# A decoder trunk on one core: ScalarE scales a step's output rows behind the high parts of keys and scores, and VectorE forms the last row sums

## The reference

```python
h = rmsnorm(x, norm_g); proj = h @ w_in            # ten projections
u = conv3(c_a * x_a) + conv_b                      # short convolution branch
y_a = (b_a * u * silu(z_a)) @ w_a_out
# retention branch: 4 heads, chunks of 128 positions, per-head decay
s = (q @ k.T) * decay_in;  o_in = s @ v
cross = (q @ state) * xi
state = state * chunk_decay + (k * zeta).T @ v     # carried from chunk to chunk
o = o_in + cross
o = o * rsqrt(mean(o * o) + EPS)                   # per row of 512
y_b = (o * silu(z_b)) @ w_b_out
x = x + (sigmoid(g_a) * y_a + sigmoid(g_b) * y_b) @ w_o
out = rmsnorm(x, final_g)
```

## Time and profile before

| | |
|---|---|
| median of three runs | 1357.13 us |
| the profiled execution's own time | 1357.46 us |
| its span | 1355.7 us |
| TensorE busy | 1344.5 us, 99% |
| VectorE busy | 1101.8 us, 81% |
| ScalarE busy | 621.2 us, 46% |
| GpSimd busy | 381.1 us, 28% |
| granted TensorE clock, mean | 0.998 of full speed |

### The profile page before, as it was taken

How to read it: one execution, slowest core, us unless ns; L and a number is a source line. 1 busy time by engine, 2 the same in 40 slices (tenths; PEclk the granted TensorE clock), 3 DMA queues, 4 the chain that set the end, 5 groups by cost and what they waited for, 6 DMA issues and landing times.

```text
span 1355.7 us, 18174 instructions
## 1 busy us (share of the span) xinstructions
PE 1344.5 (99%) x6930; PEld 1150.3 (85%) x6930; DVE 1101.8 (81%) x1179; ACT 621.2 (46%) x844; POOL 381.1 (28%) x411
## 2 busy tenths in 40 slices
PE   9999999999999999999999999999999999999997
PEld 8788888888888899888888888888888888888886
DVE  6898575688888888789999998748776998788887
ACT  7843243433333343333434443448778433434445
POOL 0100112344444554333343342225444001100002
PEclk9999999999999999999999999999999999999999
DMA  9746477877677777778888889878878699945443
GB/s 337 217 132 215 139 218 225 263 204 204 200 216 230 218 233 229 255 245 273 281 273 274 273 291 291 251 219 252 265 220 266 155 326 304 232 157 202 163 86 125
DMA packets 134630, 310.35 MB, mean 229 GB/s; under 512 B 9488, under 2 KB 54160, under 8 KB 125456
## 3 DMA queue, kind: packets, MB, share of 16 engines
q1 hardware_dynamic: 123024, 260.41, 54.4%
q0 software_dynamic: 11376, 48.76, 19.6%
q10 hardware_dynamic: 144, 0.02, 0.0%
HBM read 241.00 MB, written 59.77 MB: 222 GB/s over the span
## 4 chain that ended last, share of the span: by engine, by line
PE 91%; ACT 2%; DVE 2%; DMA 2%; issue 2%; POOL 1%; SPq 1%; POOLq 0%; ACTq 0%; DVEq 0%
PE psum L2747 13%; PE psum L2745 13%; PE psum L2748 13%; PE psum L2888 7%; PE psum L2889 7%; PE psum L2890 7%; PE psum L2663 5%; PE psum L2665 5%; PE psum L2664 5%; PE psum L2652 3%; PE psum L2655 3%; PE psum L2654 3%; PE psum L2790 2%; PE psum L2792 2%; PE psum L2791 2%
## 5 line engine op out<-in xcount | busy, mean ns | idle before, releaser
L1210 ACT ACTIVATE slots<-work 128x1024 fp32r<-128x1024 f32 (+1 forms) x182 | 182.1, 1009 | 404.8 <-PE psum L2748 147.7
L2747 PE MATMUL psum<-hc,slots 128*128 128x512 f32 x784 | 305.2, 389 | 0.0
L2745 PE MATMUL psum<-hc,slots 128*128 128x512 f32 x784 | 305.2, 389 | 0.0
L2748 PE MATMUL psum<-hc,slots 128*128 128x512 f32 x784 | 305.1, 389 | 0.0
L1503 ACT ACTIVATE last_slot<-arena 128x1024 fp32r<-128x1024 f32 x112 | 118.6, 1062 | 163.0 <-PE psum L2890 156.5
L2888 PE MATMUL psum<-last_slot 128*128 128x512 f32 (+1 forms) x452 | 175.3, 388 | 0.0
L2889 PE MATMUL psum<-last_slot 128*128 128x512 f32 (+1 forms) x452 | 175.0, 387 | 0.0
L2890 PE MATMUL psum<-last_slot 128*128 128x512 f32 (+1 forms) x452 | 175.0, 387 | 0.0
L2748 PEld LDWEIGHTS psum<-hc,slots 128*128 128x128 f32 x784 | 147.2, 188 | 30.8
L2745 PEld LDWEIGHTS psum<-hc,slots 128*128 128x128 f32 x784 | 147.2, 188 | 29.4
L2747 PEld LDWEIGHTS psum<-hc,slots 128*128 128x128 f32 x784 | 147.2, 188 | 29.3
(11 more groups left out here) (230 smaller groups left out, 2753.6 us busy)
## 6 DMA issues: line engine op xcount, KB each, us to landing
work<-w_channel SPq DMA_DIRECT2D x99, 512.0 KB, 5.7
hx<-hx_scratch SPq DMA_DIRECT2D x32, 1024.0 KB, 8.9
work<-w_channel POOLq DMA_DIRECT2D x59, 512.0 KB, 7.1
arena<-w_last SPq DMA_DIRECT2D x19, 1024.0 KB, 7.8
hx<-hx_scratch SPq DMA_DIRECT2D x32, 512.0 KB, 6.4
qk<-qk_scratch SPq DMA_DIRECT2D x32, 512.0 KB, 4.5
arena<-w_last POOLq DMA_DIRECT2D x9, 1024.0 KB, 11.2
v_raw<-value_scratch SPq DMA_DIRECT2D x32, 256.0 KB, 4.9
```

Of the source, the lines that this page charges most:

```text
L1210: nc.scalar.activation(slots[:, u % SLOTS, 0, 0:columns_of(u)], src, ACT.Copy, scale=-1.0 if negated(u) else 1.0).then_inc(w_hi, 1)
L2745: nc.tensor.matmul(bank, slot[:, 0, w], x_high, start=product in STARTS and j == 0, stop=False, skip_group_check=True)
L2747: nc.tensor.matmul(bank, slot[:, 0, w], x_low, start=False, stop=False, skip_group_check=True)
L2748: last = nc.tensor.matmul(bank, slot[:, 1, w], x_high, start=False, stop=j == 3, skip_group_check=True)
```

## The change

There are two parts. In the retention ScalarE's `o_scale_rows(s - 1)` moves, for `s` = 2 to 28, from before `score_high(s + 1)` to behind it. At the end VectorE adds tiles 0, 1, 2 and the right half of tile 3 each one `row_normed` earlier, and the two additions that make the last tile's row sum (`half_total`, `last_total`) are VectorE's; GpSimd keeps the power alone for that tile.

```diff
         def row_factored(t):
...
+            if t < 7:
+                pool.wait_ge(row_var, 4 + t)
+                pool.wait_ge(row_squared, TT + 8 + t + 1)
+                nc.gpsimd.tensor_tensor(row_sum[:, one], row_early[:, one], row_sum[:, one], ALU.add)\
+                    .then_inc(row_var, 1)
+                pool.wait_ge(row_var, 5 + t)
+            else:
+                pool.wait_ge(last_sum, last_sums_until(OUTPUT, 3) + 8)
             nc.gpsimd.tensor_tensor(row_factor[:, one], row_sum[:, one], minus_half[:, one], ALU.pow)\
                 .then_inc(row_factor_made, 1)
...
         for s in range(STEPS):
             if 2 < s + 1 < STEPS:
                 v_high(s + 1)
-            if 1 < s <= UPDATES:
-                o_scale_rows(s - 1)
             if 2 < s + 1 < STEPS:
                 score_high(s + 1)
-            if s > UPDATES:
+            if s > 1:
                 o_scale_rows(s - 1)
...
+        def half_total():
+
+            dve.wait_ge(row_squared, TT + 16)
+            dve.wait_ge(row_var, 4)
+            nc.vector.tensor_tensor(half_sum, row_early[:, 7:8], half_sum, ALU.add).then_inc(last_sum, 1)
+
+        def last_total():
+
+            dve.wait_ge(row_squared, TT + 17)
+            dve.wait_ge(last_sum, last_sums_until(OUTPUT, 3) + 7)
+            nc.vector.tensor_tensor(row_sum[:, 7:8], half_sum, row_sum[:, 7:8], ALU.add).then_inc(last_sum, 1)
...
         row_normed(0)
         row_normed(1)
+        tile_add(0)
         row_normed(2)
-        tile_add(0)
+        tile_add(1)
         row_normed(3)
-        tile_add(1)
         seventh_added()
+        tile_add(2)
         row_normed(4)
-        tile_add(2)
+        tile_add(3, slice(HALF // 2, HALF), last_bank(OUTPUT, 3))
         row_normed(5)
-        tile_add(3, slice(HALF // 2, HALF), last_bank(OUTPUT, 3))
         tile_add(3, slice(0, HALF // 2))
+        half_total()
         row_normed(6)
+        last_total()
         row_normed(7)
```

More of the change, by code:

```diff
@@ L1160, in row_factored @@
         def row_factored(t):
[L1162 to L1170, removed]
+            one = slice(t, t + 1)
+            if t < 7:
[6 more added lines that the diff above has]
+                pool.wait_ge(last_sum, last_sums_until(OUTPUT, 3) + 8)
             nc.gpsimd.tensor_tensor(row_factor[:, one], row_sum[:, one], minus_half[:, one], ALU.pow)\
```

## The result

The changed kernel takes 1368.27 us (median; 1367.84 to 1369.21 over five runs), the kernel before 1357.04 (1356.2 to 1357.75, five runs): a ratio of 1.0084, 95% interval 1.0072 to 1.0095, so it is slower by 0.8%, 11.2 us. Forecast were 1369.1 us with a range of 1366.5 to 1373.0. The profiled execution of the changed kernel has a span of 1366.5 us, 10.8 more than before.

The account below looks back on a forecast made before the run. A ScalarE/VectorE loop closed by list order was taken to set the pace, 18.42 us a round against TensorE's 18.2. 1357.46 + 12.6 (retention) - 0.6 (end) = 1369.5, less 0.33 for the median: 1369.1 us; range 1366.5 to 1373.0.

Parts of the forecast that it names:

- The loop paces, not TensorE: Retention: a ScalarE/VectorE loop closed by list order takes 18.42 us per round of four steps, TensorE 18.2.
- The rival that TensorE hides it: Retention: TensorE sets the pace and hides the scaling, only the end moves, 1356.5 us; chance 5%.
- 0.58 per loop, 22 loops: Retention: the scaling ahead of the state's high part adds 0.58 us to each of 22 loops, 12.8 us.
- Ahead of keys it lay in a gap: ScalarE in the retention: the scaling's old place cost nothing despite 11.5 us of waiting, so moving it gains nothing.
- TensorE's transposes in time: Retention: scaled rows ready 1.58 us after the decayed scores, TensorE needing them at about 1.6, a tie.
- the rival that had 7%: Retention: TensorE's transposes become late by 0.25 us each, 22 x 0.25 = 5.5 more, 1374.6 us; chance 7%.
- The stops before `update`: TensorE in the retention: it stops in every step before `update`, 0.3 to 0.9 us, released by `new_state`.
- GpSimd and VectorE don't collide in the loop: Retention: GpSimd's difference stays off the state's low part, since both hang on the state's high part and move alike.
- Before step 8: -0.2 us: Early retention, loop not closed: one step gains 0.79 and gives back 0.58, -0.2 us; later scalings elsewhere are absorbed.
- the rival of the two engines that shut each other out: Retention: GpSimd's 128x512 difference falls on VectorE's state low part each step, 20 us more, 1389 us; chance 4%.
- The end: -0.6 us: After TensorE's last matmul: power about 1.1 us earlier from earlier adds and VectorE sums; half passes the last stores, -0.6.
- the end of +0.3: Kernel's end, slow bound: 0.3 us later if a sum holds up the seventh `row_normed`, plus one semaphore more.

Follow-up runs that it names:

- e3: Changed kernel with the scaling one place later still, behind the state's high part, in steps 4 to 28; 1357.0 us, ratio 1.0 to the kernel before.
- e7: Kernel before plus an unused ScalarE 128x512 copy ahead of the scaling in steps 4 to 28; 1356.72 us, ratio 0.9998.
- e6: Kernel before plus an unused ScalarE 128x512 copy between the scores' and the state's high part, steps 4 to 28; 1369.76 us, ratio 1.0095.
- e2: Kernel before with only the end's change, `o_scale_rows` left where it was; 1356.32 us, ratio 0.9994.
- e8: Kernel before with only VectorE's tile additions one place earlier, the last totals left on GpSimd; 1356.37 us, ratio 0.9997.
- e1: Kernel before with only the retention's change, the scaling behind keys and scores, the end as before; 1369.98 us, ratio 1.0094.
- e5: Kernel before with VectorE's `o_gate` moved behind the decayed scores and the changed kernel's end; 1354.51 us, ratio 0.998.
- e9: Kernel before with only the last tile's two totals moved to VectorE, tile additions in the old order; 1356.98 us, ratio 1.0.

## Why the prediction was right, step by step

- **The loop paces, not TensorE.** Right. The distances of the loop (0.32, 0.37, 1.08, 1.15, 1.19) stand within 0.01 in after, with 0.58 put in. e3 has the same work and e7 more, and both have the old round; e6 has the slow round with the old order. The rival that TensorE hides it (1356.5) is ruled out. The Trainium skill, Perfetto Trace Analysis, "Identifying the Most-Contended Engine", has the engine with the highest occupancy optimized first, and judges TensorE's headroom by other measures than matmul busy time. By busy time that engine is TensorE, and its 99% did stay; the measured 20.72 a round shows that it was not what set the pace here.
- **0.58 per loop, 22 loops.** Right for the twenty: 0.574 each. For the two behind them the size fits (1.15), and the decayed scores of steps 28, 29 and 30 stand 5.11 and 3.33 apart for 4.55 and 2.75. But e3 loses 1.12 in the same stretch with no scaling ahead of the state's high part, so what passes that loss on is open. The distance from start to start was the price, not the row's length of 0.68: 22 x 0.68 would have been 15.0. The prediction's bounds "11.4 to 15.9 us after that 0.2" hold a slip, 23 x 0.69 less 0.2 being 15.7; its range was summed without it.
- **Ahead of keys it lay in a gap.** Right: keys still start 0.32 after the decayed scores without it, so the 11.5 us of waiting in the earlier trace rows cost nothing. e7 fills the same gap with a second instruction, free.
- **TensorE's transposes in time.** Right in the loops, where the prediction saw a tie. The waits from 941 to 1038 us, after:

```profile
PE psum L2802 <- POOL v_parts L1088: 5.8, 9, 0.7
PEld psum L2843 <- ACT o_rows L1423: 3.8, 19, 0.2
```

  PE has no row of waiting for the transposes (L2843) there, only the weight load beside them, at most 0.2. Behind the loops they were late once, by the 1.31 us at 1043.98 that is shown with e3: the rival that had 7% holds in that one step, at a cost that is within the 1.15. The stops before `update` are 0.2 us in steps without `o_gate` and 0.8 with it, in every step; 0.3 to 0.9 was said.
- **GpSimd and VectorE don't collide in the loop.** Right: in the twenty loops the state's low part stays at 1.22 to 1.23 and the scores' at 0.28.
- **Before step 8: -0.2 us, it was -0.56.** A size that was off. The step named, with the power of 1.45 us, gave 0.20 (decayed scores of step 7 to those of step 8: 5.69 before, 5.49 after). More than the rest, 0.44, came between the decayed scores of steps 4 and 5 (4.58 and 4.14 apart). Timelines there, before and then after:

```profile
915.76 1.29 POOL L1088 TENSOR_TENSOR v_parts<-v_raw,v_parts 128x512 fp32r<-128x512 f32 x1 [0.65 <-ACT v_parts L1395]
...
916.01 2.13 DVE L2078 TENSOR_TENSOR state_parts<-state,state_parts 128x1024 fp32r<-128x1024 f32 x1
```

```profile
914.70 1.29 POOL L1088 TENSOR_TENSOR v_parts<-v_raw,v_parts 128x512 fp32r<-128x512 f32 x1 [0.65 <-ACT v_parts L1395]
...
915.38 1.69 DVE L2076 TENSOR_TENSOR state_parts<-state,state_parts 128x1024 fp32r<-128x1024 f32 x1
```

  The state's low part took 2.13 us beside GpSimd's low part of the values, and 1.69 now that it starts 0.43 later against it; alone it takes 1.22. It was 0.91 longer where GpSimd's instruction had 1.04 left to run, and 0.47 where it had 0.61. That fits the rival of the two engines that shut each other out, with the other sign and at one place. The Trainium skill, SBUF — State Buffer, "Who interferes with whom", has a VectorE instruction with two inputs in SBUF contend with a GpSimd instruction that reads SBUF; the trace agrees with these numbers, but no run isolates it. Half of the 0.44 goes again one step later (4.95 for 4.73), where the scores' low part takes 0.98 us for 0.27. And the prediction had a later instruction absorbed before step 8; e6's copies, which cost 1.3 us there, show that this holds only in part.
- **The end: -0.6 us, it was -0.74, for half the reason given.** The last add did start when TensorE was done and ended 0.83 earlier against `last_slot`. But that GpSimd's two additions "leave the chain" is the step that failed: I let their going be worth 0.4, and e2, with the sums on VectorE, has its last power no earlier than e8 without (307.80 and 307.79). VectorE's sum took 0.15 where I took 0.28, but it began 0.34 after its input was ready, behind `row_normed(6)`, and the power 0.23 after that. I had named such a hold-up as the end of +0.3 and not taken it. Nor was the other half of the sum right: I let the last stores pass on half of 1.1, and they passed on 0.74 of the power's 0.93. The two errors partly cancel, so that the sum came out near is luck.
- **The total.** Retention +12.07 from its first low part (12.6 said), the end -0.74 (-0.6 said), against a median 0.8 below the forecast. The profiled execution has 0.53 less ahead of the retention as well, which is no effect of the change: e1, with the same instructions up to there, has 0.32 more than before.

## What to carry to other kernels

Look for the loop that the order of two lists closes, by following start to start from one instruction to its next self, and compare it with what the busy engine needs in the same round; here 18.42 against 18.2 us, under a busy share of 99%. Before moving an instruction, ask on which side of the loop's members it will stand: the same copies of 0.5 us cost 12.8 us at one place and nothing ahead of keys, and a wait that looks long (11.5 us) was slack. Then use the slack that is there: `o_gate` in VectorE's gap of 0.54 us gave 1.8 of the 2.5 us of e5; the rest is the end's.

## What the runs showed of the hardware

VectorE's addition of 128x1 is 0.15 to 0.16 us long, and GpSimd's next instruction that needs it starts 0.23 after it starts (1361.09 and 1361.32); GpSimd's own addition of the same size was 0.18 to 0.70 long. From the ready square to the power it was 0.40 us with the sum on VectorE and nothing ahead of it (e9), 0.56 with the sum on GpSimd (e8), and 0.57 with the sum on VectorE behind another instruction: the shorter addition saved 0.16, and the queue took it back. A 128x512 instruction on ScalarE holds back the next one for 0.53 (the copy) to 0.58 us (the scaling), though its row is 0.62 to 0.69 long.
